# Two passes over the weight tiles of a mixer unit in place of one

## The reference

```python
u = x @ w_in                      # (256, 2048) @ (2048, 20480)
a_in, q, k, v, c_in, g_in = split(u)
a = silu(layer_norm(conv31(a_val * sigmoid(a_gate)) + b))
att = three dilated window attentions, merged by their denominators
c = cb * conv3(cc * ch)
merged = sum_n sigmoid(g_in[n]) * ([a, att, c][n] @ w_branch[n])
x = layer_norm(alpha * x + merged @ w_out)
idx, w = route(x)                 # 64 experts, 8 per token
x = layer_norm(alpha * x + sum_e w_e * swiglu_e(x) + shared(x))
```

## Time and profile before

| | |
|---|---|
| three runs, median | 2239.57 us |
| lowest and highest | 2237.03 and 2244.02 us |
| the profiled execution | 2235.77 us |
| its span, first to last instruction | 2233.9 us |
| mean granted TensorE clock | 0.997 |
| TensorE busy | 2198.7 us |
| VectorE / ScalarE busy | 1043.7 / 703.1 us |
| mixer, up to the last output unit | about 1,170 us |

### The profile page before, as it was taken

One profiled execution on the slowest core, in us unless ns is written; L12 is line 12 of the kernel. 1 busy time (PEld: TensorE's weight loads), 2 busy tenths in 40 slices (PEclk: granted clock), 3 DMA queues, 4 the chain that ended last, 5 costly groups with the idle time before them and its releaser, 6 DMA issues.

```text
span 2233.9 us, 34431 instructions
## 1 busy us (share of the span) xinstructions
PE 2198.7 (98%) x14150; PEld 1694.1 (76%) x14150; DVE 1043.7 (47%) x1329; ACT 703.1 (31%) x782; POOL 50.4 (2%) x56
## 2 busy tenths in 40 slices
PE   8999999999999999999999999999999999999997
PEld 7888888888888888888889666666666666666663
DVE  5444559996585666666664322222122111222224
ACT  4333544434444444444424111111111111111112
POOL 0000000000000000000100000000000000000000
PEclk9999999999999999999999999999999999999999
DMA  8555445555355655555677599999999999999996
GB/s 266 188 188 188 145 161 184 188 187 190 114 172 188 204 189 188 187 188 185 221 245 301 244 421 421 422 422 422 422 422 422 422 422 422 422 422 422 422 421 260
DMA packets 250666, 643.37 MB, mean 288 GB/s; under 512 B 5173, under 2 KB 185397, under 8 KB 198378
## 3 DMA queue, kind: packets, MB, share of 16 engines
q1 hardware_dynamic: 249578, 635.61, 74.6%
q0 software_dynamic: 880, 6.32, 0.7%
q10 hardware_dynamic: 144, 0.52, 0.1%
HBM read 640.34 MB, written 2.10 MB: 288 GB/s over the span
## 4 chain that ended last, share of the span: by engine, by line
PE 78%; DMA 20%; DVE 1%; issue 0%; ACT 0%; DVEq 0%; SPq 0%; ACTq 0%
PE ps_proj L1524 22%; DMA ring<-in_w_up_dram 20%; PE ps_proj L1738 13%; PE ps_proj L1525 11%; PE ps_s L1779 5%; PE ps_s L1515 4%; PE ps_s L1517 2%; PE ps_t L1498 2%; PE ps_s L1498 2%; PE ps_t L1691 2%; PE ps_t L1795 2%; PE ps_proj L1795 1%; PE ps_proj L1653 1%; PE ps_proj L1691 1%; PE ps_t L1499 1%; PE ps_s L1499 1%
## 5 line engine op out<-in xcount | busy, mean ns | idle before, releaser
L1524 PE MATMUL ps_proj<-x_both,w_both 128*128 128x512 f32 x2144 | 746.4, 393 | 0.0
L1525 PE MATMUL ps_proj<-x_both,w_both 128*128 128x256 f32 x2144 | 598.3, 279 | 0.0
L942 DVE TENSOR_TENSOR w_both<-raw,w_both 128x2048 fp32r<-128x2048 f32 x196 | 472.2, 2410 | 202.8 <-ACT w_both L658 202.4
L1524 PEld LDWEIGHTS ps_proj<-x_both,w_both 128*128 128x128 f32 x2144 | 401.4, 187 | 89.8
L1738 PE MATMUL ps_proj<-ring,xt 128*64 128x256 f32 x4192 | 462.1, 379 | 6.3 <-DMA ring<-in_w_up_dram 6.1
L1738 PEld LDWEIGHTS ps_proj<-ring,xt 128*64 128x64 f32 x4192 | 301.1, 137 | 175.3 <-issue 18.2
L1525 PEld LDWEIGHTS ps_proj<-x_both,w_both 128*128 128x128 f32 x2144 | 404.3, 189 | 0.1
L658 ACT ACTIVATE w_both<-raw 128x2048 fp32r<-128x2048 f32 x196 | 373.4, 1908 | 86.0 <-PE ps_proj L1525 43.9
L1779 PE MATMUL ps_s<-ring,ht 128*64 128x512 f32 x1056 | 233.9, 595 | 0.5 <-issue 0.5
L1295 DVE SCALAR_TENSOR_TENSOR hidden<-ps_proj,slot_w,gate_sig 128x256 f32<-128x256 f32 x33 | 16.0, 484 | 365.1 <-ACT gate_sig L820 365.1
L1303 DVE TENSOR_TENSOR y_lo<-ps_s,y_hi 128x1024 fp32r<-128x1024 f32 x64 | 75.4, 1219 | 219.7 <-ACT y_hi L838 219.7
(11 more groups left out here) (293 smaller groups left out, 2295.6 us busy)
## 6 DMA issues: line engine op xcount, KB each, us to landing
raw<-in_w_in_dram SPq DMA_DIRECT2D x79, 2048.0 KB, 8.6
ring<-in_w_up_dram SPq DMA_DIRECT2D x64, 2048.0 KB, 25.0
ring<-in_w_down_dram SPq DMA_DIRECT2D x64, 2048.0 KB, 18.9
ring<-in_w_gate_dram SPq DMA_DIRECT2D x63, 2048.0 KB, 21.8
raw<-in_w_branch_dram SPq DMA_DIRECT2D x12, 2048.0 KB, 8.0
raw<-in_w_out_dram SPq DMA_DIRECT2D x8, 2048.0 KB, 9.4
ring<-in_w_gate_dram SPq DMA_DIRECT2D x4, 1024.0 KB, 21.6
ring<-in_w_up_dram SPq DMA_DIRECT2D x4, 1024.0 KB, 24.7
```

The lines of the kernel that those rows point to most:

```text
L942: nc.vector.tensor_tensor(split_lo(u, w), raw_half(u, w), split_hi(u, w).bitcast(F32), ALU.subtract).then_inc(s_lo, 1)
L1524: pe.matmul(sums[:, :], hi[:, t, :], x_both[:, :, t, :], start=(t == 0), stop=False)
L1525: ins = pe.matmul(sums[:, 0:TOK], lo[:, t, :], x_hi[:, t, :], start=False, stop=(t == KT - 1))
```

## The change

The loop over the 16 tiles of a unit becomes two loops. The first issues the 16 products of 512 columns, the second the 16 of 256. `start` (which clears the sums) stays on the first product, `stop` and the signal on the last.

```diff
                     sums = ps_proj[u.bank]
                     for t in range(KT):
                         pe.matmul(sums[:, :], hi[:, t, :], x_both[:, :, t, :], start=(t == 0), stop=False)
+                    for t in range(KT):
                         ins = pe.matmul(sums[:, 0:TOK], lo[:, t, :], x_hi[:, t, :], start=False, stop=(t == KT - 1))
                 ins.then_inc(s_mm, 1)
```

## The result

The changed kernel takes 2242.18 us (median of 20 runs, 2241.46 to 2243.78) against 2237.68 us before (20 runs, 2233.23 to 2244.02): ratio 1.0022, 95% interval 1.0016 to 1.0029. That is slower by 4.5 us, inside the 0.3% that was called no change. The profiled execution took 2243.13 us, its span is 2241.4 us, 7.5 us longer than the one shown of before.

The account below looks back on a forecast made before the run. TensorE was taken to bound the mixer, transfers the experts' second half. 2,010 pairs at 3.2 ns more gave 6.4 us, all on the path; 2239.6 + 6.4 = 2246.0 us, range 2232 to 2254.

Parts of the forecast that it names:

- no change: Whole kernel: a difference within 0.3%, 6.7 us, counts as the same; chance of same 0.50.
- That only 2,010 pairs are touched, all on the path: Mixer's edited lines: 15 pairs in each of 134 units change price, with TensorE never idle ahead of them.
- The new pair at 0.3498 us: Edited units: wide to wide plus narrow to narrow, 3.2 ns over the present 0.3466 us; 6.4 us in all.
- the wide price: Edited units: a wide-to-wide step at 0.2308 us, from 12 steps in the combining of the experts.
- Rival 1: Edited units: order is neutral, products stay at 0.230 and 0.1166 us; 0 to +2 us, chance 0.29.
- Narrow to narrow: Edited units: a step at 0.1190 us, from 50 steps in the gathering of tokens.
- The v, gate-branch and output units have their own lines and stay: Mixer units outside the edited lines: they keep their code and were given no change in time.
- Rival 2: Edited units: uniform blocks lock into the output units' slower pace, 6.7 ns a pair, 13.5 us; chance 0.18.
- Theory A: From the experiments: switching narrow to wide costs, settled blocks do not; a block leaves the alternating stretch behind it slow.

Follow-up runs that it names:

- the first experiments: Blocks of 8, 4 and 2 wide and narrow products in place of 16, edited from the changed kernel: 2244.67, 2247.04 and 2241.89 us.
- beside the last: Blocks in the output units and the last four column groups only, other units as in the kernel before: 2239.52 us, ratio 1.0000.

## Why the prediction came out as it did

The time lay in the range, 3.8 us under the forecast, and the 4.5 us of slowing were inside the 0.3% that had the chance of 0.50. The range alone proves little: all 20 runs of before lie in it too. Of the 3.8 us, 1.9 come from the base: three runs had the median 2239.57, twenty have 2237.68. The other 1.9 are the change, +6.4 forecast and +4.5 measured, and that this is so near is luck. In the profiles the edited units pay 2.7 us, under half of the 6.4, and the units that the prediction left out pay more than that.

1. **That only 2,010 pairs are touched, all on the path**: the counts and the path held. TensorE is not idle ahead of the lines, the starts come in blocks, the shift of 7.4 us arrives whole at the experts and stays.
2. **The new pair at 0.3498 us**: over-sized. In a unit, the 15 wide steps take 3.428 us and the 15 narrow ones 1.793 in the trace, 0.3481 a pair; with the two remaining switches the unit has 20 ns more, not 48. The term that was mis-sized is the wide price: 12 steps at 0.2308, taken from bursts of 8 products. Those bursts are too short to settle. The first six of these steps are 236, 228, 233, 231, 226 and 227 ns in the trace of before, within 1 ns the ones at the head of a block in the changed kernel; the mean hid that the last two had come down already. A settled wide product is 0.2267 (every product wide), a settled narrow one 0.120, and their sum is 0.3467: what the alternating order costs. Rival 1 was right that order is neutral, but with other single prices than it named, and only once a block has settled. The switch is what costs, 20 ns each in blocks of 8 or more. Narrow to narrow was right: 0.1190 forecast, 0.1195 measured.
3. **"The v, gate-branch and output units have their own lines and stay"**: wrong, and worth 4.3 us of the profiled 7.4. They keep their code and lose their pace. Rival 2 had the pace (0.3533) and the fact that order can lead into it, and the wrong place: the grouped blocks never ran at it, and those that alternate behind them did.
4. **The profiled 7.4 us and the 4.5 of the medians.** The execution profiled of before was 1.9 us faster than its median of 20 runs, the changed one 0.95 slower than its own. Kernels whose 134 units alternate spread widely (2233.6 to 2248.5 over 22 runs beside the first experiments; 2234.5 to 2250.1 over 11 beside the last; 2233.7 to 2248.4 over six with blocks in the output units alone), those with blocks in these units little (2.3 us, 2.0, 2.4, 2.6, 2.6 for blocks of 16, 8, 4, 2 and everywhere). That fits with pauses that throw the pace of alternating stretches, and with block units that settle to 5.567 whatever came before. For the slowest runs, 2247 to 2250, it is argued only: none of them had a profile. At 0.107 us a unit, 15 us over the fastest would take about 140 of the 200 alternating units, an estimate from the two paces; the most that a pause was seen to start is 14 in a row.

What the slow pace is in the engine was not found. Theory A stands as a description: what starts it, what keeps it, what ends it.

## What to carry to other kernels

Price an order of products by long settled streams and count the switches, not by a few steps from a short burst. Before calling unedited code unchanged, compare its starts in both traces: the pace of a stream on TensorE can depend on what ran ahead of it. If a stretch alternates two widths, either leave it all so or group all of it: with blocks of 4, 8 or 16, each alternating unit right behind a grouped one ran slow here.

## What the runs showed of the hardware

- An alternating stream of 512- and 256-column fp32r products, a weight load each, has two stable paces at the same granted clock of 1.00: 0.3467 and 0.3533 us a pair. Either lasts over 200 pairs and more. At the fast one the steps are 230 and 117 ns throughout; at the slow one they repeat every three pairs (before, from 1118.9 us on: wide 236, 232, 240 ns, narrow 114, 118, 120).
- A block of 16 and 16 (or 8 and 8, or 4 and 4) ahead of it leads into the slow one each time it was seen; a pause leads into either, not the same in each execution.
- Blocks of 2 and 2 left the first v units at 5.547 us and the branch-weight units behind other blocks of 2 at 5.65: the handing on is not a matter of "block or not" alone. This was not followed up.
- A wide product costs 0.230 us ahead of a narrow one at the fast pace, and 0.2267 in an unbroken stream; the narrow one makes up for it exactly, 0.1167 and 0.120.
